# RMSNorm statistics of a hybrid decoder step: tokens on the partitions in five columns instead of four groups of 130, and the sample operations behind two tiles

## The reference, cut to what matters

```python
def rmsnorm(x, g, eps=RMS_EPS):
    xf = x.astype(jnp.float32)
    y = xf * lax.rsqrt(jnp.mean(xf * xf, axis=-1, keepdims=True) + eps)
    return (y * g.astype(jnp.float32)).astype(x.dtype)
...
        u = rmsnorm(h, p['norm_g'][l, 0]) * (1 + sc_m) + sh_m
...
        h = h + gt_m * rmsnorm(out, p['norm_g'][l, 1])
        u = rmsnorm(h, p['norm_g'][l, 2]) * (1 + sc_f) + sh_f
...
        h = h + gt_f * rmsnorm(out, p['norm_g'][l, 3])
```

## Time and profile before

| | |
|---|---|
| median of three executions | 3162.73 us (3162.24 to 3166.47) |
| profiled execution | 3162.33 us, its span 3160.6 us |
| TensorE matmul / weight load busy | 94% / 89% of the span |
| VectorE / ScalarE / GpSimd busy | 50% / 33% / 40% |
| mean granted TensorE clock | 0.967 of 2.4 GHz |

### The profile page before, as it was taken

How to read it: one execution, slowest core, us unless ns; L and a number is a source line. 1 busy time by engine, 2 the same in 40 slices (tenths; PEclk the granted TensorE clock), 3 DMA queues, 4 the chain that set the end, 5 groups by cost and what they waited for, 6 DMA issues and landing times.

```text
span 3160.6 us, 75176 instructions
## 1 busy us (share of the span) xinstructions
PE 2963.8 (94%) x30609; PEld 2799.9 (89%) x30609; DVE 1572.8 (50%) x2369; ACT 1048.2 (33%) x2007; POOL 1275.0 (40%) x890
## 2 busy tenths in 40 slices
PE   6998999988989998899999899989999899899997
PEld 5997999978878886799999699879999799799997
DVE  3436666035157777466621352466660344576612
ACT  3224333234342333333322443343332322433321
POOL 3443544342332223344444163434443344354542
PEclk9998999989999999899999899999999899899998
DMA  7552333642420002323345232433336353133232
GB/s 260 161 185 65 93 93 100 204 119 89 133 54 4 3 3 52 120 82 94 91 148 169 88 107 81 147 111 91 94 99 205 104 161 102 54 95 93 87 92 76
DMA packets 465050, 332.69 MB, mean 105 GB/s; under 512 B 19850, under 2 KB 435544, under 8 KB 464546
## 3 DMA queue, kind: packets, MB, share of 16 engines
q1 hardware_dynamic: 460824, 325.23, 33.6%
q10 hardware_dynamic: 4010, 4.22, 0.6%
HBM read 319.62 MB, written 10.20 MB: 104 GB/s over the span
## 4 chain that ended last, share of the span: by engine, by line
PE 82%; DVE 10%; issue 3%; ACT 2%; DMA 2%; POOL 1%; DVEq 0%; SPq 0%; ACTq 0%; POOLq 0%
PE bank L1542 46%; PE bank L1550 23%; PE bank L1990 3%; PE bank L1565 2%; PE bank L1503 2%; DMA ada_pro<-in_ada_w_dram 1%; DVE h L2453 1%; PE bank L1571 1%; PE bank L1840 1%; DVE proj L2398 1%; PE bank L1632 1%; DVE mmt L2738 1%; DVE rstd L2344 0%; DVE xf L2504 0%; ACT w_hi L909 0%
## 5 line engine op out<-in xcount | busy, mean ns | idle before, releaser
L732 POOL TENSOR_TENSOR w_lo<-w_raw,w_hi 128x1024 fp32r<-128x1024 f32 x404 | 1019.6, 2524 | 1217.9 <-ACT w_hi L909 1196.9
L1542 PE MATMUL bank<-u_hi,w_hi 128*128 128x260 f32 x4064 | 833.3, 286 | 21.1 <-ACT w_hi L909 14.7
L1542 PE MATMUL bank<-u_lo,w_hi 128*128 128x260 f32 x4064 | 823.4, 284 | 0.0
L1542 PEld LDWEIGHTS bank<-u_hi,w_hi 128*128 128x128 f32 x4064 | 625.2, 189 | 36.6 <-issue 24.8
L1542 PEld LDWEIGHTS bank<-u_lo,w_hi 128*128 128x128 f32 x4064 | 627.8, 189 | 1.8
L909 ACT ACTIVATE w_hi<-w_raw 128x1024 fp32r<-128x1024 f32 x402 | 424.4, 1056 | 478.4 <-PE bank L1550 234.5
L1550 PE MATMUL bank<-u_hi,w_lo 128*128 128x260 f32 x4064 | 528.2, 282 | 0.0
L1550 PEld LDWEIGHTS bank<-u_hi,w_lo 128*128 128x128 f32 x4064 | 502.5, 187 | 1.7
L1542 PE MATMUL bank<-hid_hi,w_hi 128*128 128x260 f32 x1664 | 337.6, 284 | 0.0
L1542 PE MATMUL bank<-hid_lo,w_hi 128*128 128x260 f32 x1664 | 335.0, 283 | 0.0
L2888 DVE TENSOR_TENSOR csb<-proj 128x520 f32 (+1 forms) x42 | 30.0, 714 | 486.4 <-ACT proj L974 486.4
(11 more groups left out here) (456 smaller groups left out, 3926.9 us busy)
## 6 DMA issues: line engine op xcount, KB each, us to landing
w_raw<-in_ffn_w_up_dram SPq DMA_DIRECT2D x176, 512.0 KB, 3.7
ada_raw<-in_ada_w_dram SPq DMA_DIRECT2D x132, 512.0 KB, 4.7
w_raw<-in_ffn_w_down_dram SPq DMA_DIRECT2D x64, 448.0 KB, 4.0
w_raw<-in_sconv_w_in_dram SPq DMA_DIRECT2D x48, 512.0 KB, 5.6
w_raw<-in_ffn_w_down_dram SPq DMA_DIRECT2D x32, 512.0 KB, 4.0
ada_pro<-in_ada_w_dram SPq DMA_DIRECT2D x6, 2048.0 KB, 21.4
w_raw<-in_rwkv_w_rkv_dram SPq DMA_DIRECT2D x24, 512.0 KB, 4.4
w_raw<-in_gla_w_in_dram SPq DMA_DIRECT2D x24, 512.0 KB, 4.4
```

The lines of the kernel that those rows point to most:

```text
L732: pool.tensor_tensor(w_lo[:, s, :, :], w_raw[:, s, :, :], w_hi[:, s, :, :].bitcast(F32), ALU.subtract).then_inc(lo_done, 1)
L1542: pe.matmul(tile_ps[slot][half][0:width, 0:HALF], w_hi[:, s, k, 0:width], x[:, k0 + k, half * HALF:(half + 1) * HALF], start=start and k = ...
```

## The change

`token_sums` turns the operands round. Five matmuls per tile hold 128 squares' tokens as the stationary operand (128x128) and stream one column of `ones`; token t of group g lands on partition t, column g, of bank 4. The fifth group is the last 128 tokens, 392 to 519, so that the samples are its last eight partitions. Only the first matmul of the first tile has the start flag. `root` and the reciprocal work on 5 columns instead of 130. `spread_rstd` holds one column of `rstd`, repeated 128 times, as stationary operand and streams the identity: first 8 columns for the samples, then four times 128 columns, all into one bank. So `times_rstd` is one multiplication of 512 columns. In the post-norms the second and third sample operation move from ahead of the tiles to behind the multiplications of tiles 0 and 1, ahead of the first addition into `h`.

```diff
-        rstd_ps = (bank[5][:, 0:SPAN], bank[7][:, P:P + TG])
+        rstd_ps = (bank[5][:, 0:TP], bank[7][:, P:P + NS])
+        TOKENS = tuple(slice(g * P, (g + 1) * P) for g in range(TP // P)) + (slice(T - P, T),)
+        NTOK = len(TOKENS)
...
-                act.activation(std[:, 0:TG], sums_ps[:, 0:TG], ACT.Sqrt, bias=eps_col[:, 0:1],
+                act.activation(std[:, 0:NTOK], sums_ps[:, 0:NTOK], ACT.Sqrt, bias=eps_col[:, 0:1],
...
             def token_sums(squares, first, final):
-                for g in range(NG):
-                    mm = pe.matmul(sums_ps[g * QUAD:(g + 1) * QUAD, 0:TG], ones[:, :], squares[:, g * TG:(g + 1) * TG],
-                                   start=first, stop=final)
+                for g, tokens in enumerate(TOKENS):
+                    mm = pe.matmul(sums_ps[:, g:g + 1], squares[:, tokens], ones[:, 0:1], start=first and g == 0,
+                                   stop=final and g == NTOK - 1)
                 return mm
...
             def spread_rstd(norm):
                 pe.wait_ge(rstd_ready, norm + 1)
-                for g in (NG - 1,) + tuple(range(NG - 1)):
-                    out = rstd_ps[0][:, g * TG:(g + 1) * TG] if g < NG - 1 else rstd_ps[1]
-                    mm = pe.matmul(out, ident[:, g * QUAD:g * QUAD + 1].to_broadcast([P, P]), rstd[:, 0:TG],
-                                   start=True, stop=True)
-                    if g >= NG - 2:
-                        mm.then_inc(rstd_turned, 1)
+                pe.matmul(rstd_ps[1], rstd[:, NTOK - 1:NTOK].to_broadcast([P, P]), ident[:, P - NS:P], start=True, stop=True)\
+                  .then_inc(rstd_turned, 1)
+                for g, tokens in enumerate(TOKENS[:-1]):
+                    mm = pe.matmul(rstd_ps[0][:, tokens], rstd[:, g:g + 1].to_broadcast([P, P]), ident[:, :],
+                                   start=True, stop=True)
+                mm.then_inc(rstd_turned, 1)
...
-                dve.reciprocal(rstd[:, 0:TG], std[:, 0:TG]).then_inc(rstd_ready, 1)
+                dve.reciprocal(rstd[:, 0:NTOK], std[:, 0:NTOK]).then_inc(rstd_ready, 1)
...
             def times_rstd(out, x):
-                dve.tensor_tensor(out[:, 0:SPAN], x[:, 0:SPAN], rstd_ps[0], ALU.mult)
-                return dve.tensor_tensor(out[:, SPAN:TP], x[:, SPAN:TP], rstd_ps[1][:, 0:TP - SPAN], ALU.mult)
+                return dve.tensor_tensor(out[:, 0:TP], x[:, 0:TP], rstd_ps[0], ALU.mult)
...
                     link(dve.tensor_tensor(s8[:, 0], proj_x[:, :, TP:T], rs, ALU.mult))
-                    link(dve.tensor_tensor(s8[:, 0], s8[:, 0], mod[:, 2 * KT:3 * KT, 1:NSEQ], ALU.mult))
-                    link(dve.tensor_tensor(h[:, :, TP:T], h[:, :, TP:T], s8[:, 0], ALU.add))
                     spread_all(p["norm"])
                     for k in range(KT + 1):
                         if k < KT:
                             step[0] += 1
                             times_rstd(proj_x[:, k, :], proj_x[:, k, :]).then_inc(dve_step, 1)
+                        if k == 1:
+                            link(dve.tensor_tensor(s8[:, 0], s8[:, 0], mod[:, 2 * KT:3 * KT, 1:NSEQ], ALU.mult))
+                            link(dve.tensor_tensor(h[:, :, TP:T], h[:, :, TP:T], s8[:, 0], ALU.add))
```

More of the change, by code:

```diff
@@ L2343, in inverse_root @@
                 dve.wait_ge(std_done, norm + 1)
-                dve.reciprocal(rstd[:, 0:TG], std[:, 0:TG]).then_inc(rstd_ready, 1)
+                dve.reciprocal(rstd[:, 0:NTOK], std[:, 0:NTOK]).then_inc(rstd_ready, 1)
             def spread(norm):
                 dve.wait_ge(rstd_turned, 2 * norm + 1)
-                return rstd_ps[1][:, TP - SPAN:TG].unsqueeze(1).to_broadcast([P, KT, NS])
+                return rstd_ps[1].unsqueeze(1).to_broadcast([P, KT, NS])
             for i in range(GT // PRO_T):
```

## The result

The changed kernel takes 3240.35 us (median of four executions, 3237.51 to 3243.72) against 3163.56 us (3162.24 to 3166.47) on the same chip: 76.8 us or 2.4% slower, ratio 1.0241, 95% interval 1.0228 to 1.0253. Its profiled execution is the slowest of the four, 3243.72 us with a span of 3242.0 us, 81.4 us longer than the span before; so its trace has to explain 4.6 us more than the medians differ by. The mean granted clock fell from 0.967 to 0.948.

The account below looks back on a forecast made before the run. TensorE's loads at 1.2 GHz, instead of VectorE, were taken to bound the norms' statistics; 60 + 7 + 0.4 + 3 = 70.4 us on 3162.3 gave 3232.7 us, own range 3212 to 3248, chance 0.67.

Parts of the forecast that it names:

- The sums decide: Pre-norm statistics: ten passes a tile, each with a load, take 0.2145 us a pass, 2.14 us a tile at 1.2 GHz.
- The clock stays low through the sums: Pre-norm statistics: the clock falls to 1.2 GHz and doesn't rise until `gemm_pair` streams, so TensorE passes VectorE as the bound.
- the two lines of the earlier trace: Old profile: 8-column passes for 2.3 of 3.4 us kept 2.4 GHz; spread and transposes for 2.88 of 3.40 us stayed at 1.2.
- rival 2: In the sums the clock falls but a load takes 0.112 us at either clock: +3 us a pair, about 3181 us; chance 0.08.
- Per pair +10.0: Each of six post-norm and pre-norm pairs with `ada_columns` in the statistics takes 10.0 us more, 60 us together.
- the seventh: The pair at layer 3's mixer, without `ada_columns` in its statistics, takes +7 us.
- Rival 3: In some pairs of norms the clock stays up or comes back midway: 3165 to 3210 us, say 3190; chance 0.08.
- Root and reciprocal: In each norm, 5 columns instead of 130 save 0.18 us on the root and 0.75 on the reciprocal, together 0.93 us.
- Spread and multiplication: In the norms, ten spread passes bring all factors 0.23 to 0.43 us later; one multiplication saves 0.06 us a tile.
- Sample operations: In post-norms, moving two operations behind two tiles shortens VectorE's stall to some 0.6 us; first addition 0.4 us sooner.
- Prologue: Prologue sums take 9 us at 2.4 GHz or 17 at 1.2, partly hidden by arriving data: +3 us, between 0 and 8.
- the sum: Whole kernel: 60 for six pairs, 7 for the seventh, 0.4 for the last norm, 3 for the prologue, 70.4 us.

## Why the prediction was right, point by point

- **The sums decide: right.** At 1.2 GHz a tile's ten loads take 2.21 us and one of them 0.33, so (2.21 - 0.33) / 9 = 0.21 us each, where 0.2145 was put down from the two first loads of the earlier trace rows. At 2.4 GHz the twenty passes behind the last two blocks take 2.29 us, 0.11 each, as in the earlier trace rows. The tile of 277.80 and its `ada_columns` of 280.03 take 3.24 us up to the next tile's sums (3.01 said: 2.23 for the sums and 1.01 for the columns instead of 2.14 and 0.87). The statistics as a whole took 20.9 us where 20.7 was said, or 20.2 with the 0.5 us of the first passes; some eight passes ran before the clock fell at 271.9.
- **The clock stays low through the sums: right.** It fell as the sums ran and stayed at 0.50 until `gemm_pair` had streamed for 5.7 us. This was the choice between the two lines of the earlier trace rows, and neither was a stretch of loads with next to nothing streamed: the first holds 1.07 us of passes with 130 columns, the second 2.10 us of the old spread, 130 columns a pass. The kernel with 102 columns against that with one (3180 against 3240 us, same loads) makes it more than a reading. The Trainium skill (TensorE: Matmul & The Clock Gate, "What's actually happening") says that the gate goes by how busy the engine has been; in this kernel a TensorE occupied for 20.13 of 20.20 us was granted 1.2 GHz.
- **Load at either clock:** rival 2, a load that keeps its speed, is out by those 0.21 us. The same page ("LDWEIGHTS (loading the stationary operand)") would give an estimate of 107 ns for 128 columns; the trace agrees at 2.4 GHz (0.11 us) and shows twice that at 1.2 (0.21 us).
- **Per pair +10.0:** measured 10.4, 8.6, 8.5, 10.7, 9.4 and 10.6, on average 9.7; the seventh +6.5 where +7 was said. This is from root to root. It leaves out that the first root comes 0.85 us later behind the product, and that `gemm_pair` starts 0.54 us sooner behind the second root; both are in the forecast's 10.0 and nearly cancel. Rival 3, norms that escape, did not come in any pair: each had a stretch of 24 to 41 us at 0.50.
- **Root and reciprocal:** the reciprocal takes 0.19 us (0.22 said). The root takes 0.27 us on 5 columns, not 0.185: the row it was taken from is another function of ScalarE with another destination. The term is 0.10 + 0.78 = 0.88 instead of 0.93.
- **Spread and multiplication:** eight passes of 128 columns in 1.14 us, plus 0.24 for the sample factors ahead of them; the single multiplication starts every 0.60 to 0.67 us and takes 0.68. As said. But from the first addition on VectorE no longer sets the pace, so what the single multiplication saves there lies off the path.
- **Sample operations:** the stall of 1.62 us became 0.51 (0.6 said), because GpSimd's operation ended at 266.80 + 2.38 = 269.18, or 263.8 without the 5.4 us of the prologue (263.9 said). The first addition came at 264.15 without those 5.4 us, 0.57 us sooner than before (0.4 said). The move is worth 6.9 us over all in the changed kernel.
- **Prologue:** mis-sized, +5.4 instead of +3, inside the 0 to 8 that were given. The sums ran for 14.4 us, between the 9 at 2.4 GHz and the 17 at 1.2 that were put down; the clock was at 0.50 from 29.5 on. The kernel before waited for arriving data three times in this stretch, 5.92 us in all; the changed one doesn't wait for data there, so no more of the sums could be hidden than that. In the kernel before, the second of the three waits, and in the changed one the sums:

```profile
39.71 2.65 PE L1655 MATMUL bank<-ada_pro,cT 128*32 128x128 f32 x64 [3.11 <-DMA ada_pro<-in_ada_w_dram]
...
26.46 14.43 PE L1594 MATMUL bank<-ones,csb 128*128 128x1 f32 x80
```

- **What was missed:** the sum had nothing for the stretches between the norms. Layer 1's mixer took 9.2 us more and the others 1.9, +11.1 in all. The profiled executions differ by 81.4 us where the sum had 70.4, and that is these 11.1, with the prologue's 2.4 too little and the pairs' 2.3 too much about even. The medians differ by 76.8, so the time is 7.6 above the forecast, in the upper part of its range. So the mechanism was right, and what the forecast lacks is a silent step: it took it that a stretch whose code is unchanged keeps its time. In the trace it doesn't; how much of the 9.2 us other executions have isn't known.

## What to carry to other kernels

Turning a reduction by TensorE round, so that the data is the stationary operand and a column of ones is streamed, makes every 128 tokens cost a load and streams next to nothing; here TensorE was busy all the time and its clock stood at 1.2 GHz, and 0.9 us saved in the small operations was paid with 11 us. Price such a stage at both clocks, and look in the trace for a stretch of the same kind that had to win the clock back, not one that only had to keep it. When a small operation takes several times what its columns need, look for the other engine's long operation beside it; behind two tiles it cost a seventh.

## What the runs showed of the hardware

- With one column streamed under each load TensorE was occupied for 20.13 of 20.20 us at a granted clock of 0.50, `ada_columns` included, and with 32 columns for 19.27 of 19.30 us at 0.50. The same loads with 102 columns in each pass had 0.99 in the later part of the sums.
- A pass with a load of 128 fp32 columns and one streamed column took 0.11 us at 2.4 GHz and 0.21 us at 1.2 GHz.
- An fp32 pass that streams 260 columns under a new 128x128 operand took 4.58 / 20 = 0.23 us at 2.4 GHz, twice what the 260-column passes of the split products take (0.12, from 0.24 us between rows of two). I had expected the same.
- In one pause of 3.13 us the clock fell in the traces of five kernels and stayed in those of six, with the work around it unchanged; where it fell, the stretch took 6 to 10 us more than before the change.
- A VectorE operation on 64 columns took 1.62 us beside a GpSimd operation of 2.35 us, both ending together, and 0.22 us behind it.
